# One phase for the first mixing layer's norm and projection, with the filter network and the short convolution placed inside it

## The reference

```python
z = rmsnorm(h, mix_norm) @ mix_w_in            # 512 x 1024 by 1024 x 3328
y_a = rwkv7_bidir(z[..., :RWKV_COLS], ...)     # 1792 columns
y_b = hyena_bidir(z[..., RWKV_COLS:], ...)     # 1536 columns
h = h + concatenate([y_a, y_b]) @ mix_w_out

def hyena_bidir(z, ...):
    u = dwconv_centred(z, short_w, short_b)    # three taps along the tokens
    x0, x1, v = u[..., :C], u[..., C:2 * C], u[..., 2 * C:]        # C = 512
    h = hyena_filters(L, ...)                  # depends on weights alone
    kern = concatenate([h[:, 0], zeros, flip(h[1:, 1])])
    s = v * x1
    y = irfft(rfft(s, n=2 * L) * rfft(kern, n=2 * L))[:, :L]
    return (y + s * bias) * x0

def hyena_filters(L, w1, b1, w2, b2, w3, b3, w4, freq):
    hdn = sin(freq * (feats @ w1 + b1))        # 512 x 64, three such layers
    hdn = sin(freq * (hdn @ w2 + b2))
    hdn = sin(freq * (hdn @ w3 + b3))
    h = (hdn @ w4).reshape(L, 2, C) * exp(-t * deltas)
    return h * rsqrt(sum(h * h, axis=(0, 1)) + EPS)
```

## Time and profile before

| | |
|---|---|
| median of 3 runs | 3489.85 us (3485.0 to 3491.21) |
| profiled execution | 3489.5 us |
| its span in the trace | 3487.7 us |
| PE busy | 3120.9 us (89%) |
| DVE busy | 1628.6 us (47%) |
| ACT busy | 1314.7 us (38%) |
| POOL busy | 89.5 us (3%) |
| TensorE's granted clock, mean | 0.925 of 2.4 GHz |

### The profile page before, as it was taken

How to read it: one execution, slowest core, us unless ns; L and a number is a source line. 1 busy time by engine, 2 the same in 40 slices (tenths; PEclk the granted TensorE clock), 3 DMA queues, 4 the chain that set the end, 5 groups by cost and what they waited for, 6 DMA issues and landing times. The chain is left out here.

```text
span 3487.7 us, 47358 instructions
## 1 busy us (share of the span) xinstructions
PE 3120.9 (89%) x19958; PEld 2433.7 (70%) x19958; DVE 1628.6 (47%) x2294; ACT 1314.7 (38%) x2020; POOL 89.5 (3%) x190
## 2 busy tenths in 40 slices
PE   7948688779999889889999878889999898889999
PEld 5824477767777667667777666567888775568887
DVE  2152555545445346745454336654333348543333
ACT  3210434324333333544333333654424235545151
POOL 0000000001000000000000010000000010100000
PEclk9959777789999999999999989999999899989999
DMA  3110100026444222225444222002323130013222
GB/s 126 63 40 24 41 3 2 3 74 190 162 146 141 89 85 85 76 83 178 164 142 149 76 70 81 1 12 74 100 94 101 52 123 3 1 61 97 97 97 85
DMA packets 223521, 286.67 MB, mean 82 GB/s; under 512 B 7555, under 2 KB 163459, under 8 KB 217172
## 3 DMA queue, kind: packets, MB, share of 16 engines
q1 hardware_dynamic: 214580, 229.73, 20.8%
q0 software_dynamic: 7680, 51.91, 4.3%
q10 hardware_dynamic: 1056, 2.10, 0.2%
HBM read 281.62 MB, written 2.10 MB: 81 GB/s over the span
## 5 line engine op out<-in xcount | busy, mean ns | idle before, releaser
L231 DVE TENSOR_TENSOR weights_low_all<-weights,weights_high_all 128x2048 fp32r<-128x2048 f32 x196 | 449.9, 2295 | 672.1 <-ACT weights_high_all L225 668.4
L225 ACT CAST weights_high_all<-weights 128x2048 fp32r<-128x2048 f32 x196 | 373.5, 1906 | 646.6 <-PE ps L239 636.3
L237 PE MATMUL ps<-ffn_h_high,weights_high_all 128*128 128x512 f32 x704 | 277.8, 395 | 0.9 <-DVE weights_low_all L231 0.9
L239 PE MATMUL ps<-ffn_h_high,weights_low_all 128*128 128x512 f32 x704 | 274.4, 390 | 0.0
L238 PE MATMUL ps<-ffn_h_low,weights_high_all 128*128 128x512 f32 x704 | 274.4, 390 | 0.0
L237 PE MATMUL ps<-mlp_h_high,weights_high_all 128*128 128x512 f32 x512 | 201.0, 393 | 3.1 <-DVE weights_low_all L231 1.8
L239 PE MATMUL ps<-mlp_h_high,weights_low_all 128*128 128x512 f32 x512 | 199.5, 390 | 0.0
L238 PE MATMUL ps<-mlp_h_low,weights_high_all 128*128 128x512 f32 x512 | 199.5, 390 | 0.0
L237 PE MATMUL ps<-weights_high_all,mlp_hid_high 128*128 128x512 f32 x512 | 199.2, 389 | 0.0
L238 PE MATMUL ps<-weights_low_all,mlp_hid_high 128*128 128x512 f32 x512 | 199.2, 389 | 0.0
L239 PE MATMUL ps<-weights_high_all,mlp_hid_low 128*128 128x512 f32 x512 | 199.2, 389 | 0.0
(11 more groups left out here) (548 smaller groups left out, 6373.2 us busy)
## 6 DMA issues: line engine op xcount, KB each, us to landing
mod_w<-in_w_mod POOLq DMA_DIRECT2D x48, 1024.0 KB, 5.2
weights<-in_ffn_w_up SPq DMA_DIRECT2D x88, 512.0 KB, 5.0
weights<-in_w_mlp_in SPq DMA_DIRECT2D x32, 1024.0 KB, 5.5
weights<-in_w_mlp_out SPq DMA_DIRECT2D x32, 1024.0 KB, 5.0
weights<-in_ffn_w_down SPq DMA_DIRECT2D x24, 768.0 KB, 4.4
weights<-in_mix_w_in SPq DMA_DIRECT2D x13, 1024.0 KB, 5.1
weights<-in_na_w_qkv SPq DMA_DIRECT2D x12, 1024.0 KB, 5.2
weights<-in_w_in SPq DMA_DIRECT2D x12, 1024.0 KB, 5.8
```

Source lines behind the costliest of these rows:

```text
L225: nc.scalar.copy(st.high[s][:], st.raw[s][:]).then_inc(st.high_done, 1)
L231: nc.vector.tensor_tensor(st.low[s][:], st.raw[s][:], st.high[s][:], ALU.subtract).then_inc(st.split_done, 1)
L237: nc.tensor.matmul(out, lh, rh, start=start, stop=False)
L239: return nc.tensor.matmul(out, ll, rh, start=False, stop=stop)
```

## The change

The norm and both projections become one phase (`mix_in_phase`) on the classes `Norm` and `Up`, in a new class `MixIn`. The short convolution is computed straight from the banks of the 6 Hyena groups, by ACT (centre tap) and DVE (the two others). The filter network's matmuls, the transposes of s and the sums of squares go between the weight groups (`beside_tensor`): a layer after groups 0, 2 and 4, the 8 output matmuls after 6 and 7, transposes after 8 and 9, squares after 8 and 10. The squares, sums and differences of the filters move from DVE to GpSimd, as does the issue of the small loads and of the forward tables. The inverse tables get buffers of their own and are loaded at the start of the Hyena phase, the inverse transform runs frequency tile by frequency tile (the outer loop is f, not k), and ACT instead of DVE applies the scale. The first groups of `mix_w_out` may be loaded within the projection.

```diff
-        while self.issued < min([upto, len(self.groups)] + self.stops[:1]):
+        while self.issued < min(upto, len(self.groups)):
...
+class MixIn(Up):
...
+    N_CONV = 6
+    FILTER_IN, FILTER_OUT, SQUARES, TURNS = (0, 2, 4), (6, 7), (8, 10), {8: (0, 1, 2), 9: (3,)}
...
+        self.decay = y.work[:, 0:4, :]
+        self.taken = y.work[:, 4:8, :]
...
+    def free(self, pe, g, j):
+        if g < self.N_CONV:
+            pe.wait_ge(self.taps, 2 * (2 * g + j) + 2)
+        else:
+            pe.wait_ge(self.copied, 2 * (g - self.N_CONV) + j + 1)
+    def square(self, t, q):
+        return self.y.u[:, 8 + 2 * (t % 2) + q, :]
+    def pool(self, pool, d, turned):
+        nc, y = self.nc, self.y
+        for dst, src in ((self.feats[:], d["k_featsT"]), (self.w1[:], d["hy_f_w1"][0]), (self.w23[:, 0, :], d["hy_f_w2"][0]),
+                         (self.w23[:, 1, :], d["hy_f_w3"][0]), (self.w4[:], d["hy_f_w4"][0]),
+                         (self.decay, d["k_decay"].rearrange("(t p) c -> p t c", p=P))):
+            nc.gpsimd.dma_start(dst, src).then_inc(self.small, 16)
+        pool.wait_ge(turned, KT)
+        pool.wait_ge(self.product, TT)
+        for t in range(TT):
+            a, b = (self.taken[:, 2 * (t % 2) + q, :] for q in range(2))
+            pool.wait_ge(self.decayed, 2 * t + 2)
+            if t >= 2:
+                pool.wait_ge(self.sq_sum, t - 1)
+            for q, side in enumerate((a, b)):
+                nc.gpsimd.tensor_tensor(self.square(t, q), side, side, ALU.mult).then_inc(self.squared, 1)
+            if t == 0:
+                pool.wait_ge(self.squared, 2)
+                nc.gpsimd.memset(b[0:1, :], 0.0).then_inc(self.cleared, 1)
+                pool.wait_ge(self.cleared, 1)
+            nc.gpsimd.tensor_tensor(y.h_sum[:, t, :], a, b, ALU.add).then_inc(self.joined, 1)
+            nc.gpsimd.tensor_tensor(y.h_dif[:, t, :], a, b, ALU.subtract).then_inc(self.joined, 1)
+        pool.wait_ge(self.joined, 2 * TT)
+        for q, n in enumerate(("k_dft_c", "k_dft_s")):
+            nc.gpsimd.dma_start(y.dft[q], d[n].rearrange("(t p) c -> p t c", p=P)).then_inc(y.tabs, 16)
...
+    def tensor(self, pe, norm):
+        self.behind(pe, norm)
+        self.beside_tensor(pe, 0)
+        for g in range(1, self.n):
+            self.group(pe, g, lambda j: self.free(pe, g - 2, j) if g >= 2 else None)
+            self.beside_tensor(pe, g)
+    def beside_tensor(self, pe, g):
+        nc, ps, y = self.nc, self.cx.ps, self.y
+        if g in self.FILTER_IN:
+            l = self.FILTER_IN.index(g)
+            if l:
+                pe.wait_ge(self.sin_done, l)
+            else:
+                pe.wait_ge(self.small, 6 * 16)
+            nc.tensor.matmul(ps[0:64, 4 + l, :], self.w1[:] if l == 0 else self.w23[:, l - 1, :],
+                             self.feats[:] if l == 0 else self.hdn[:], start=True, stop=True).then_inc(self.layer_sum, 1)
+        if g in self.FILTER_OUT:
+            first = 2 * self.FILTER_OUT.index(g)
+            if first == 0:
+                pe.wait_ge(self.sin_done, 3)
+            for t in (first, first + 1):
+                for q in range(2):
+                    n = 2 * t + q
+                    if n >= 4:
+                        pe.wait_ge(self.decayed, n - 3)
+                    nc.tensor.matmul(ps[:, 4 + n % 4, :], self.hdn[:, t * P:(t + 1) * P], self.w4[:, q * HY:(q + 1) * HY],
+                                     start=True, stop=True).then_inc(self.out_sum, 1)
+        if g in self.TURNS:
+            pe.wait_ge(self.product, TT)
+            pe.wait_ge(self.decayed, 2 * TT)
+            for t in self.TURNS[g]:
+                if t == 3:
+                    pe.wait_ge(self.s_done, 1)
+                for k in range(TT):
+                    mm = nc.tensor.transpose(ps[:, self.turn_bank(t), k * P:(k + 1) * P], y.u[:, 4 + k, t * P:(t + 1) * P],
+                                             self.cx.ident[:])
+                mm.then_inc(self.turned, 1)
+        if g in self.SQUARES:
+            first = 2 * self.SQUARES.index(g)
+            pe.wait_ge(self.decayed, 2 * TT)
+            for t in (first, first + 1):
+                pe.wait_ge(self.squared, 2 * t + 2)
+                for q in range(2):
+                    for k in range(TT):
+                        mm = nc.tensor.matmul(ps[:, 7, k:k + 1], self.square(t, q)[:, k * P:(k + 1) * P], self.cx.ones[:, 0:1],
+                                              start=(t == 0 and q == 0 and k == 0), stop=(t == TT - 1 and q == 1 and k == TT - 1))
+                mm.then_inc(self.sq_sum, 1)
...
+    def scalar(self, act):
+        nc, ps, y = self.nc, self.cx.ps, self.y
+        for g in range(self.n):
+            split_ahead(nc, self.st, act, self.g0 + g + 1, "high")
+            if g - 1 in self.FILTER_IN:
+                act.wait_ge(self.arg_done, self.FILTER_IN.index(g - 1) + 1)
+                nc.scalar.activation(self.hdn[:], self.arg[:], ACT.Sin).then_inc(self.sin_done, 1)
+            if g - 1 in self.TURNS:
+                for t in self.TURNS[g - 1]:
+                    act.wait_ge(self.turned, t + 1)
+                    nc.scalar.copy(y.s_tm[:, t, :], ps[:, self.turn_bank(t), :]).then_inc(self.s_done, 1)
+            for j in range(2):
+                self.wait_sum(act, g, j)
+                sums, n = ps[:, self.bank(g, j), :], 2 * g + j
+                if g < self.N_CONV:
+                    nc.scalar.activation(y.u[:, n, :], sums, ACT.Identity, bias=column(self.cx, "hy_b", n),
+                                         scale=column(self.cx, "hy_w1", n)).then_inc(self.centre, 1)
+                else:
+                    nc.scalar.copy(self.z[:, n - 2 * self.N_CONV, :], sums).then_inc(self.copied, 1)
+        act.wait_ge(self.sq_sum, TT)
+        nc.scalar.activation(y.scale[:], ps[:, 7, 0:TT], ACT.Sqrt, bias=self.cx.rope_inv[:, 2:3]).then_inc(self.root, 1)
...
+    def vector(self, dve):
+        nc, ps, y, cx = self.nc, self.cx.ps, self.y, self.cx
+        link = Link(nc, self.ctx, dve, "mi_order")
+        for g in range(self.n):
+            split_ahead(nc, self.st, dve, self.g0 + g + 1, "low")
+            if g - 1 in self.FILTER_IN:
+                l = self.FILTER_IN.index(g - 1)
+                dve.wait_ge(self.layer_sum, l + 1)
+                link(nc.vector.tensor_scalar(self.arg[:], ps[0:64, 4 + l, :], column(cx, f"hy_f_b{l + 1}", 0)[0:64],
+                                             column(cx, "hy_f_freq", 0)[0:64], ALU.add, ALU.mult))
+                less_whole_turns(nc, link, self.arg[:], self.whole[:])
+                nc.vector.sem_inc(self.arg_done, 1)
+            if g - 1 in self.FILTER_OUT:
+                first = 2 * self.FILTER_OUT.index(g - 1)
+                for t in (first, first + 1):
+                    for q in range(2):
+                        n = 2 * t + q
+                        dve.wait_ge(self.out_sum, n + 1)
+                        if t >= 2:
+                            dve.wait_ge(self.joined, 2 * (t - 1))
+                        nc.vector.tensor_tensor(self.taken[:, 2 * (t % 2) + q, :], ps[:, 4 + n % 4, :], self.decay[:, t, :],
+                                                ALU.mult).then_inc(self.decayed, 1)
+            if g < self.N_CONV:
+                for j in range(2):
+                    sums, n = ps[:, self.bank(g, j), :], 2 * g + j
+                    dve.wait_ge(self.centre, n + 1)
+                    nc.vector.scalar_tensor_tensor(out=y.u[:, n, 1:L], in0=sums[:, 0:L - 1], scalar=column(cx, "hy_w0", n),
+                                                   in1=y.u[:, n, 1:L], op0=ALU.mult, op1=ALU.add).then_inc(self.taps, 1)
+                    dve.wait_ge(self.taps, 2 * n + 1)
+                    nc.vector.scalar_tensor_tensor(out=y.u[:, n, 0:L - 1], in0=sums[:, 1:L], scalar=column(cx, "hy_w2", n),
+                                                   in1=y.u[:, n, 0:L - 1], op0=ALU.mult, op1=ALU.add).then_inc(self.taps, 1)
+            if g == self.N_CONV - 1:
+                dve.wait_ge(self.taps, 4 * self.N_CONV)
+                for k in range(TT):
+                    nc.vector.tensor_tensor(y.u[:, 4 + k, :], y.u[:, 4 + k, :], y.u[:, 8 + k, :], ALU.mult).then_inc(self.product, 1)
+        dve.wait_ge(self.root, 1)
+        nc.vector.reciprocal(y.scale[:], y.scale[:])
...
+            mix.tensor(pe, norm)
+        @block.scalar
+        def _(act):
+            norm.scalar(act)
+            mix.scalar(act)
+        @block.vector
+        def _(dve):
+            norm.vector(dve)
+            mix.vector(dve)
...
+        idft = [sb("idft_" + n, [P, TT, L]) for n in ("c", "s")]
...
+            @block.sync
+            def _(sp):
+                for q, n in enumerate(("k_idft_c", "k_idft_s")):
+                    sp.dma_start(idft[q][:], d[n].rearrange("(t p) c -> p t c", p=P)).then_inc(inverse, 16)
...
+                pe.wait_ge(inverse, 32)
+                for f in range(TT):
```

(23 more changed lines are left out.)

305 lines of the change are left out of this document (82 added, 223 removed).

## The result

The changed kernel takes 3414.3 us (median of four runs, 3408.07 to 3416.18) against 3489.7 for the kernel before (3485.0 to 3491.21): a ratio of 0.9783, 95% interval 0.9766 to 0.98. The forecast was 3414.0 with 3402 to 3432. The span falls from 3487.7 to 3412.1, by 75.6 us, and TensorE's mean granted clock rises from 0.925 to 0.938.

A forecast was written before the change was run, and what follows sets the result against it. PE bounds the kernel, losing time to waits and narrow half-clock work. The new schedule ends the Hyena part at 286.5 against 361.66, 75.2 us less: 3489.5 - 75.2 = 3414.3, forecast as 3414, range 3402 to 3432.

The forecast's parts named there:

- Start: Projection's beginning: products start at 27.4, cold start costs 2.0 us, group 0 ends at 42.5 against 46.0.
- Groups: Projection groups 1 to 12: 12 x 10.87 = 130.4 us, phase boundary of 1.8 us gone, reaching 172.9.
- Insertions: Filter matmuls, transposes and squares between groups: 19.2 us of work, plus 4 for two clock falls at the squares, reaching 196.1.
- Between the phases: From PE's last projection sum to the Hyena phase: copy, table load, root and inversion, about 2.9 us, reaching 199.0.
- Hyena phase: Start of the forward transform after the phase gap: a cold start costing 2.3 us.
- Transforms and end: Forward transform 55.2 us, inverse 27.5 without a gap, closing operations 2.5; Hyena part ends at 286.5 against 361.66.
- What was costed at nothing: DVE's work moved into the groups, GpSimd's operations (about 1.26 us each for 512 columns) and table loads: 0 us.
- Rival A: The clock is kept at the gaps and the squares: 4 + 2.0 + 2.3 us less, 3406; chance 0.25.
- B: Rival: the clock falls at more insertions, up to 8 falls instead of 2; 3422 to 3443 at worst; chance 0.15.
- C: Rival: the network still waits, a step misplaced or GpSimd over 2.6 us; 26 us of waits, 3440; chance 0.07.
- D: Rival: slower than before, insertions keep the clock low through the groups; up to 130 us more, 3545; chance 0.02.

The follow-up runs named there:

- third set: The changed kernel, unedited, measured again beside the last set of runs: 3411.6 us, ratio 0.9779, stage 244.16 us.
- Norm apart: Changed kernel with the norm in a phase of its own again, ahead of the projection, and group 0 as an ordinary group: 3415.2 us, ratio 0.9805.
- squares spread: Changed kernel with the one-column passes 16 each behind groups 8, 9, 10 and 11 instead of 32 each behind 8 and 10: 3405.8 us, ratio 0.9764.
- added and busy: The squares added kernel plus five unread 512-column products around the first transposes: 3398.1 us, ratio 0.9744.
- Inverse tables late: Changed kernel asking for the inverse tables only when the last forward sums are made, as in the kernel before: 3421.3 us, ratio 0.9819.
- Sums on VectorE: Changed kernel with GpSimd's 17 operations on the filters (squares, sums, differences) moved to VectorE behind groups 7 and 9: 3411.1 us, ratio 0.9781.
- network last: Changed kernel with the filter network, its transposes and squares all behind the last weight group, same instructions: 3444.6 us, ratio 0.9887.
- turns first: Changed kernel with the passes over the squares moved from behind groups 8 and 10 to 9 and 11, twelve transposes alone behind 8: 3411.4 us, ratio 0.9782.
- squares added: Changed kernel with GpSimd adding the eight tiles of squares into one, which TensorE sums by 4 matmuls behind group 10: 3398.6 us, ratio 0.975.

## Why the prediction was right

The profiled execution gives 3414.2; the prediction's sum was 3414.3. The schedule was right; that the sum is right to 0.1 us is luck, since two terms of 2 us were off in opposite directions and the rest alone varies by 5 us. Step by step:

- *Start:* first product at 27.4, measured 27.01; group 0 ended at 42.5, measured 42.05 plus half of a pair of hand-overs, some 42.7. The start was cold, as taken: the products come 0.43 us apart until about 32.7, then 0.226. It cost 2.6 us (15.04 from the first product to the first hand-over, 12.4 at the high clock) where 2.0 was taken, and began 0.4 earlier. The reason given, a fall of the clock in the idle time behind the transposes, is not what the profiled execution shows: its transposes come 0.213 us apart and the products behind them are slow from the first; no stretch at the high rate shows before them. The third set's execution does show a fall, at 27.9, and started 1 us cheaper. (The forecast's price rests on the earlier trace rows: nine slow products from 32.78 to 36.78, where it says ten; the 2 us lost are right.) *Norm apart* gives the worth of this step as 2.5 us.
- *Groups:* 130.4, measured 130.6 (12 times 10.88). The boundary of 1.8 us is gone.
- *Insertions:* 19.2 for the work and 4 for the clock, 23.2. Measured 25.3, the mis-sized term. The three layers cost 1.22, 1.24 and 1.24, the output matmuls 3.89 and 3.90: 11.5 instead of 9.5 and 1 of edges. The transposes cost 1.8, as forecast. The squares cost 3.63 a block, 7.3 instead of 6.9: half the cold price was the right end. The two falls cost 3.2 and 1.6, 4.7 together instead of 4, at the places named.
- *Between the phases:* 2.9, measured 2.7.
- *Hyena phase:* a cold start of 2.3 was forecast and none came: the first 16 products take 7.11 us. This is the step that failed, and it made up for the 2.1 us that the insertions were over. Its premise, that a pause of some 3 us lets the clock fall, holds for some kernels and not for others: the same pause cost 0 in the changed kernel, 1.6 in *squares spread*, 1.7 in *norm apart* and 3.0 in *added and busy*.
- *Transforms and end:* 55.2 and 27.5 without a gap, 2.5 for the end. Measured 55.0 (201.28 to 256.28) and 29.9 to the end. *Inverse tables late* shows that the gap was worth 10.1 us, 8.35 plus 2.3 in the forecast.
- *What was costed at nothing:* DVE, GpSimd (1.02 to 1.28 us an operation, 1.26 forecast, and 3.50 for one pair of squares beside a split of VectorE, 2.03 otherwise) and the tables delayed no one. *Sums on VectorE* and GpSimd's trace bear that out.

Rival A, the clock kept, was right in one of its four places, the start of the forward transform; at the start and behind both blocks the clock was low. *Squares spread* comes to A's 3406 (3405.8), but by chance: it removes the two falls behind the squares and has cold starts at both ends. B and C did not occur; PE idles before none of L1335, L1344 and L1354. Nor did D: a group without an insertion takes 10.88 us, the high clock's price. Where the network stands is worth 33 us (*network last*), more than the 26 of rival C, as at half clock the matmuls and the squares double too.

On the clock, the row of the kernel before stood against a rule of the Trainium skill, that transposes don't engage the full clock ("TensorE: Matmul & The Clock Gate", "Part 4: PE-mode transpose"). The runs side with the row. Twelve transposes alone brought no fall (*turns first*, *squares added*), 32 one-column passes alone did behind group 10. And in *sums on VectorE* the clock rises within the first transposes, with nothing ahead of them but 20 us in which PE stood idle; the last four come faster than those before (each row holds two):

```profile
22.35 0.64 PE L707 MATMUL ps<-ident,hy_h_dif 128*128 128x128 f32 x2
22.78 0.57 PE L707 MATMUL ps<-ident,hy_h_sum 128*128 128x128 f32 x2
23.19 0.38 PE L707 MATMUL ps<-ident,hy_h_dif 128*128 128x128 f32 x2
```

So for the transposes of this kernel the rule does not hold: here 3.2 us of them, from 19.96 on, raised the clock. The same page says in "Part 1: The HAM clock gate (the "warmup" mystery)" that the watch over TensorE runs freely and does not start with the kernel. The four costs of one pause agree with that, but why a given kernel falls on one side or the other I can't tell from these traces, and it stays open: in three executions that reached group 8 up to 1 us apart the unedited kernel showed the same falls behind groups 8 and 10 and none at the transform, and different ones at the start.
